# Attention values of two heads in the two column halves of the array, with probabilities moving and y arriving turned

## The reference

```python
# 8 query heads of 64, 2 key/value heads (4 query heads share one), blocks of 128 tokens
# latent tokens see: key blocks t-1, t, t+1 of the latents (|distance| <= 128) + the 256 context keys
# context tokens see: the 256 context keys
s = (q @ k.T) * 64 ** -0.5               # masked
m = max(s, sink); p = exp(s - m)
y = (p @ v) / (sum(p) + exp(sink - m))   # the sink adds to the sum and has no value
...
y_mix = sigmoid(h @ w_gm) * (ym @ w_br_m) + sigmoid(h @ w_ga) * (ya @ w_br_a) + sigmoid(h @ w_gr) * (yr @ w_br_r)
```

## Time and profile before

| | |
|---|---|
| three runs | 2885.79, 2887.33, 2889.2 us |
| median | 2887.33 us |
| span of the profiled execution | 2889.5 us |
| TensorE busy | 2786.0 us (96%) |
| VectorE busy | 1287.6 us (45%) |
| ScalarE busy | 1009.6 us (35%) |
| GpSimd busy | 1113.4 us (39%) |

### The profile page before, as it was taken

The page is one execution under the profiler, slowest core; times in us unless marked ns, Lnnn a source line. Parts: engine busy times, 40 slices in busy tenths (PEclk is TensorE's granted clock), DMA queues, the critical chain, the costliest instruction groups (busy, mean ns, idle before and its releaser), DMA issues. The chain is left out here.

```text
span 2889.5 us, 43951 instructions
## 1 busy us (share of the span) xinstructions
PE 2786.0 (96%) x17300; PEld 2431.1 (84%) x17300; DVE 1287.6 (45%) x2843; ACT 1009.6 (35%) x1864; POOL 1113.4 (39%) x976
## 2 busy tenths in 40 slices
PE   7999899999999998999999999989999999899998
PEld 4888788999998897888888878877988888888887
DVE  4554537524453135333333546645625441344446
ACT  4333236533332224222222343324633332333332
POOL 2333231153333333433433444332153345365555
PEclk9999999999999999999999999999999999999999
DMA  5111210022213143111111331131022222522223
GB/s 236 59 59 62 86 66 23 16 92 88 88 74 117 59 154 124 70 62 59 73 59 59 118 117 59 52 109 67 16 99 97 94 74 85 192 88 102 88 99 112
DMA packets 39370, 249.54 MB, mean 86 GB/s; under 512 B 4480, under 2 KB 4864, under 8 KB 13568
## 3 DMA queue, kind: packets, MB, share of 16 engines
q1 hardware_dynamic: 36288, 236.25, 22.9%
q10 hardware_dynamic: 2880, 10.49, 0.9%
HBM read 236.23 MB, written 10.49 MB: 85 GB/s over the span
## 5 line engine op out<-in xcount | busy, mean ns | idle before, releaser
L2333 POOL TENSOR_TENSOR w_rest<-raw,w_head 128x512 fp32r<-128x512 f32 (+1 forms) x634 | 831.2, 1344 | 930.3 <-ACT w_head L1372 910.7
L941 PE MATMUL psum_products<-h_head,w_head 128*128 128x512 f32 (+2 forms) x2288 | 819.6, 358 | 3.8 <-DVE h_rest L1809 2.2
L941 PE MATMUL psum_products<-h_rest,w_head 128*128 128x512 f32 (+2 forms) x2288 | 803.9, 351 | 0.0
L941 PE MATMUL psum_products<-h_head,w_rest 128*128 128x512 f32 (+2 forms) x2288 | 803.9, 351 | 0.0
L941 PEld LDWEIGHTS psum_products<-h_head,w_head 128*128 128x128 f32 (+1 forms) x2288 | 428.9, 187 | 65.1 <-DVE h_rest L1809 3.4
L941 PEld LDWEIGHTS psum_products<-h_rest,w_head 128*128 128x128 f32 (+1 forms) x2288 | 428.5, 187 | 62.1 <-issue 0.8
L941 PEld LDWEIGHTS psum_products<-h_head,w_rest 128*128 128x128 f32 (+1 forms) x2288 | 429.6, 188 | 57.3 <-issue 1.5
L1372 ACT ACTIVATE w_head<-raw 128x1024 fp32r<-128x1024 f32 (+1 forms) x321 | 320.4, 1044 | 399.6 <-PE psum_products L941 350.7
L941 PE MATMUL psum_products<-w_head,h_head 128*128 128x256 f32 x1408 | 403.5, 287 | 1.6 <-DVE h_rest L1872 1.6
L941 PE MATMUL psum_products<-w_rest,h_head 128*128 128x256 f32 x1408 | 391.7, 278 | 0.0
L941 PE MATMUL psum_products<-w_head,h_rest 128*128 128x256 f32 x1408 | 391.5, 278 | 0.0
(11 more groups left out here) (278 smaller groups left out, 3793.6 us busy)
## 6 DMA issues: line engine op xcount, KB each, us to landing
raw<-in_stream SPq DMA_DIRECT2D x182, 1024.0 KB, 4.8
mods_mid<-in_stream SPq DMA_DIRECT2D x10, 1024.0 KB, 9.6
raw<-in_stream SPq DMA_DIRECT2D x16, 512.0 KB, 3.5
residual<-stage ACTq DMA_DIRECT2D x16, 512.0 KB, 2.6
stage<-residual SPq DMA_DIRECT2D x14, 512.0 KB, 4.7
mods_b<-in_stream SPq DMA_DIRECT2D x5, 1024.0 KB, 24.0
mods_a<-in_stream SPq DMA_DIRECT2D x3, 1024.0 KB, 13.8
x_in<-in_x SPq DMA_DIRECT2D x4, 512.0 KB, 8.7
```

Source lines behind the costliest of these rows:

```text
L941: return nc.tensor.matmul(o, a, b, start=start, stop=stop)
L2333: G.tensor_tensor(wl[:, s["sp"] % 2, a:b], place_of(s)[:, a:b], wh[:, s["sp"] % 2, a:b].bitcast(F32), ALU.subtract).then_inc(*ev.mark("poo ...
```

## The change

The values of two heads are made together. The items are reordered so that head g and head g + 4, which belong to different value heads, follow one another. The value block of 64 columns is now stationary, in the lower half of the array's columns for the first head and in the upper half for the second; the 128 turned probabilities move. The output is y turned: partitions are the 128 columns of y for the two heads, the free dimension is the tokens. So the four transposes of y and their copy go. The reciprocal must now stand along the tokens: VectorE writes it 64 times side by side (128x64 for each head, `a_r_rows`), TensorE turns this 128x128 block once for each pair, ScalarE copies it (`a_r_cols`), and VectorE multiplies the pair's y by it (128x128). `a_pt` gets a third buffer. The rows of `w_br_a` are reordered on the host to match. The loop has n + 3 ticks instead of n + 4.

```diff
-        heads = [(t, hd) for t in tiles for hd in range(AH)]
-        ticks("attend", AH * len(tiles) + 4, fill, 12 * len(pairs(ctx)) - 6, l=l,
-              heads=heads, banks=lambda i: int(tile_ends(heads, i)))
+        heads = [(t, g + 4 * half) for t in tiles for g in range(4) for half in range(2)]
+        ticks("attend", AH * len(tiles) + 3, fill, 12 * len(pairs(ctx)) - 6, l=l, heads=heads)
...
+                        pair = (i_ - 4) // 2 if i_ >= 4 and i_ % 2 == 0 else None
+                        if pair is not None:
+
+                            pe.wait_ge(*ev.at("ard", l, i_ - 3))
+                            pe.wait_ge(*ev.at("apt", l, i_ - 3))
+                            nc.tensor.transpose(psm[:, 3, P:2 * P], arb[:, pair % 2, :], c("ident")).then_inc(
+                                *ev.mark("pe", "arT", l, pair))
...
+                            if i_ >= 5 and i_ % 2:
+                                pe.wait_ge(*ev.at("arc", l, (i_ - 5) // 2))
...
-                        if 3 <= i_ <= n + 2:
...
-                            for m, kt_ in enumerate(keys):
-                                last = mm(psm[:, 4, 0:AD], apt[:, j % 2, m * P:(m + 1) * P],
-                                          av[:, kt_, lo:lo + AD], m == 0, m == len(keys) - 1)
-                            last.then_inc(*ev.mark("pe", "apv", l, j))
...
+                        if pair is not None:
+                            t, _ = st["heads"][2 * pair]
+                            pe.wait_ge(*ev.at("apt", l, 2 * pair + 1))
+                            if pair >= 1:
+                                pe.wait_ge(*ev.at("ay", l, pair - 1))
+                            keys = akeys(t)
                             for m, kt_ in enumerate(keys):
+                                for half in range(2):
+                                    lo = half * AD
+                                    last = mm(psm[lo:lo + AD, 4, 0:P], av[:, kt_, lo:lo + AD],
+                                              apt[:, (2 * pair + half) % 3, m * P:(m + 1) * P],
+                                              m == 0, m == len(keys) - 1)
+                            last.then_inc(*ev.mark("pe", "apv", l, pair))
...
+                        if i_ >= 4 and i_ % 2 == 0:
+
+                            pair = (i_ - 4) // 2
+                            act.wait_ge(*ev.at("arT", l, pair))
+                            if pair >= 1:
+                                act.wait_ge(*ev.at("ay", l, pair - 1))
+                            nc.scalar.activation(arc[:], psm[:, 3, P:2 * P], ACT.Copy).then_inc(
+                                *ev.mark("act", "arc", l, pair))
...
-                            V.reciprocal(small[:, s2 + 5:s2 + 6], small[:, s2 + 4:s2 + 5]).then_inc(
+                            pair, half = divmod(i_ - 2, 2)
+                            if pair >= 2:
+                                dve.wait_ge(*ev.at("arT", l, pair - 2))
+                            V.reciprocal(arb[:, pair % 2, half * AD:half * AD + AD],
+                                         small[:, s2 + 4:s2 + 5].broadcast_to((P, AD))).then_inc(
                                 *ev.mark("dve", "ard", l, i_ - 2))
...
-                            V.tensor_scalar(ay[:, t % 2, hd * AD:(hd + 1) * AD], psm[:, 4, 0:AD],
-                                            small[:, s0 + 5:s0 + 6], None, ALU.mult).then_inc(
-                                *ev.mark("dve", "ay", l, j))
+                        if i_ >= 4 and i_ % 2 == 0:
+                            pair = (i_ - 4) // 2
+                            t, hd = st["heads"][2 * pair]
+                            dve.wait_ge(*ev.at("apv", l, pair))
+                            dve.wait_ge(*ev.at("arc", l, pair))
+
+                            V.tensor_tensor(ya[:, t, hd, :], psm[:, 4, 0:P], arc[:], ALU.mult).then_inc(
+                                *ev.mark("dve", "ay", l, pair))
```

More of the change, by code:

```diff
@@ L110, in param_places @@
     return place, n
-def tile_ends(heads, i):
-    return i >= 4 and heads[i - 4][1] == AH - 1
 def make_plan():
@@ L685, in backbone @@
         kh, kr = [Region(6 * 1024 * i)(n, [P, 2, TOK], F32R) for i, n in enumerate(("a_k_head", "a_k_rest"))]
-        R = Region(12 * 1024 + 64)
-        ya = Region(R.off)("a_y_turned", [P, TILES - 1, 4, P])
+        R = Region(12 * 1024)
+        ya = Region(R.off)("a_y_turned", [P, TILES, 4, P])
         qs = R("a_q_split", [P, TILES, AH, P], F32R)
@@ L691, in backbone @@
         asb = R("a_s", [P, 3, 640])
-        apt = R("a_pt", [P, 2, 640])
-        ay = R("a_y", [P, 2, 512])
+        apt = R("a_pt", [P, 3, 640])
+        arb = R("a_r_rows", [P, 2, P])
+        arc = R("a_r_cols", [P, P])
         tga = R("a_tg", [P, 3, 2, TOK])
@@ L903, in yT_of @@
         def yT_of(br, kt, t):
-            if br != "a" or t == TILES - 1:
+            if br != "a":
                 return yT[:, 0:kt, t * P:(t + 1) * P]
@@ L1586, in _ @@
                             act.wait_ge(*ev.at("apT", l, j))
-                            if j >= 2:
-                                act.wait_ge(*ev.at("apv", l, j - 2))
-                            nc.scalar.activation(apt[:, j % 2, 0:n1], psm[:, 2, 0:n1], ACT.Copy).then_inc(
+                            if j >= 3:
+                                act.wait_ge(*ev.at("apv", l, (j - 3) // 2))
+                            nc.scalar.activation(apt[:, j % 3, 0:n1], psm[:, 2, 0:n1], ACT.Copy).then_inc(
                                 *ev.mark("act", "apt", l, j))
                             if nk > 512:
-                                nc.scalar.activation(apt[:, j % 2, 512:640], psm[:, 3, 0:P], ACT.Copy).then_inc(
+                                nc.scalar.activation(apt[:, j % 3, 512:640], psm[:, 3, 0:P], ACT.Copy).then_inc(
                                     *ev.mark("act", "apt", l, j))
+                        if i_ >= 4 and i_ % 2 == 0:
[5 more added lines that the diff above has]
+                                *ev.mark("act", "arc", l, pair))
                         if i_ < n:
@@ L1605, in _ @@
                                                      *ev.mark("act", "ap", l, i_))
[L1606 to L1612, removed]
                 elif kind == "rqk_sb":
@@ L2442, in layout @@
         w = g[name][s["l"], row:row + s["kt"] * P]
+        if name == "w_br_a":
+            w = w.reshape(2, 4, AD, -1).transpose(1, 0, 2, 3).reshape(4 * P, -1)
         w = np.concatenate([w[:, a:a + n] for a, n in cols], 1)
```

7 lines of the change are left out of this document (removed).

## The result

The changed kernel takes 2896.14 us (median of 10 runs, 2893.86 to 2900.85) against 2887.75 us for the one before (10 runs, 2885.79 to 2892.13). The ratio is 1.0027, with a 95% interval of 1.0019 to 1.0034: it is slower by 8.4 us.

A forecast was written before the change was run, and what follows sets the result against it. TensorE was taken to set the pace: work of -20.1 us and waits of +30.8 us sum to +10.7 us, which on the earlier kernel's median of 2887.3 gives 2898 us; range 2880 to 2912.

The forecast's parts named there:

- A value record at 0.055: TensorE's value products: each of 640 new records takes 0.055 us with two halves at once, 35.2 us in all.
- The switch at 0.33: TensorE entering and leaving the split array: 0.33 us for each of 40 pairs, less 0.08 already paid, 10.0 us.
- nearly free: Rival at the value groups: 0.046 us a record and no switch cost, sum -8.3 us, 2879 us; chance 0.17.
- dear: Rival at the value groups: loads bound them, 0.08 us a record, switch dearer, 16 us more, 2914 us; chance 0.08.
- no overlap: Rival at the value products: halves don't run together, 0.11 us a record, 35 us more, 2933 us; chance 0.08.
- The work at -20.1: TensorE's work: 65.3 us of value records removed, 35.2 added, 10.0 for switches, together -20.1 us.
- The reciprocal: VectorE's reciprocal, 64 elements instead of one: 7 ns for each further element, 0.48 us more, about 0.63 in all.
- rival of a cheap reciprocal: Rival at VectorE's wide reciprocal: 7 ns is scatter, 24 waits are 0.48 us shorter, no change, 2887 us; chance 0.15.
- The wait: Odd ticks without weight piece: the reciprocals' transpose starts 2.62 us after scores end (T), TensorE ready at 1.20, waiting 1.42.
- Where: Second attention stretch some 11 us longer, with 14 of the 22 waits; the first about as long as before.
- Weight loads: TensorE's full-row loads of 64 columns: under the skill's rule they don't overlap products, another 41 us, 2939 us.
- Under cover: ScalarE's added block copies, ahead of an exponential needed two ticks later, are hidden by TensorE's 93.9 of 97 us against 63.7.

The follow-up runs named there:

- e4_turn: Changed kernel with all value products of the lower half made first, then the upper half's, instead of alternating: 2913.94 us, ratio 1.0082 to the kernel before.
- e7_before_odd: Kernel before the change, with its weight pieces placed behind odd ticks first: 2892.42 us, ratio 1.0012 to the kernel before.
- e5_behind_odd: Changed kernel with weight pieces behind odd ticks first and the transpose of the reciprocals moved behind the values: 2870.23 us, ratio 0.9936 to the kernel before.
- e1_narrow: Changed kernel with the reciprocal writing one of its 64 columns, the others constant (y not the reference's): 2885.27 us, ratio 0.999 to the kernel before.
- e2_odd: Changed kernel with a weight piece behind every odd tick and the remainder behind even ones: 2872.77 us, ratio 0.9942 to the kernel before.

## Why the prediction was right

2898.0 was forecast and 2896.14 came, by the mechanism forecast. The number alone would not show it, since the range of 2880 to 2912 also held no change at all (2887); the waits, their place and the experiments do. Step by step:

- **A value record at 0.055.** The group of 20 lasts from 2053.74 to 2054.99, 1.25 us; 20 x 0.055 and the lag of 0.13 behind it are 1.23. Groups of 8, 16 and 20 (0.59, 1.02, 1.25) separate the two: 0.055 a record, and a lag of 0.15. e4_turn shows that groups of 16 and 20 need the halves to alternate for this.
- **The switch at 0.33.** Ahead of the group the five transposes take 0.64 (2053.10 to 2053.74) instead of 0.55, so 0.09. With 0.15 behind it, and 0.34 from the first weight product to the second where the next takes 0.23, so 0.11, the three lags read from quarters of the array return with halves, 0.35 together. The rivals that priced the halves otherwise (nearly free, dear, no overlap) fall with these two.
- **The work at -20.1.** TensorE's busy time fell by 12.0 in records whose ends are modelled, and some of it passed at the lower clock, which settles little. e7_before_odd against e5_behind_odd gives 22.2, with the waits left and the slow clock about even.
- **The reciprocal.** The tile's row in the changed kernel (shortest/median/longest ns):

```profile
L2215 DVE RECIPROCAL a_r_rows<-small x80: 535/543/553, 438.0 to 2099.5; 128x64 f32<-128x64 f32 x80
```

  543 - 153 = 390 ns for 63 elements are 6.2 ns each; 7 had been read. The added time is 0.39 us where I had 0.48. The Trainium skill (VectorE: DVE Perf Modes, "First, the fixed hardware budget"), read as eight cycles an element, gave an estimate of 0.53 for the added time; the trace is below that. The rival of a cheap reciprocal was wrong in its premise, and e1_narrow shows what it would have given: 2885 us, where it said 2887.
- **The wait.** The transpose of the reciprocals starts at T + 2.46 where T + 2.62 was forecast: 0.09 of the difference is the reciprocal, 0.09 the way from VectorE to TensorE (0.06, not 0.15). VectorE's start (T + 0.20) and its 1.66 us up to the reciprocal were as read. The wait is then 1.26, not 1.42. It divides into 0.70 ahead of the scores (shown as 0.53) and 0.56 ahead of the transpose (shown as 0.40). Twenty-two waits shorter by 0.16 are 3.5 us, which would make the forecast +7.2; +8.4 was measured.
- **Where.** +11 was forecast for the second layer and nothing for the first; +9.5 and, with the clock up, -1.7 came. The sizes differ by about what the wait was over-read: 14 x 0.16 = 2.2 and 8 x 0.16 = 1.3. VectorE was forecast busy for some 80 us in the second stretch; it is 72.6.
- **Weight loads.** In the second window loads are busy for 66.17 us and products for 81.33, in 97: together half as much again as the window. Full-row loads do overlap products here. The Trainium skill (TensorE: Matmul & The Clock Gate, Part 3: Packing small matmuls) lets a load overlap only when its row group differs; this trace doesn't bear that out, and the 41 us that this rule would add did not appear.

What the prediction did not see is how far ScalarE's weight conversions reach, and that the clock can fall behind the waits at a loop's end (1.5 us in the profiled execution). "Under cover" holds for the changed kernel, but once pieces stand in odd ticks, ScalarE's copies are late (6.2 us of waits in e2_odd, 8.7 in e5_behind_odd). Ten of these twelve waits stand behind two weight conversions; placing them elsewhere wasn't tried, so what that would give is open.

## What to carry to other kernels

Work of two items merged into one tick leaves the other tick empty: ask what engine was running under the work that left, and put filler there (here moving weight pieces turned +8 us into -15, with not one instruction less). A cost on a second engine is worth what its cover leaves open: 0.39 us of reciprocal was worth 11 us over 80 heads where only some ticks were covered, and nothing measurable where all odd ticks were. When a change and a placement interact, measure all four combinations, since the placement alone made the old kernel about 4 us slower. When two loops are compared, check that both ends stand behind the same work and at the same clock: here this moved 8.0 to 9.5.

## What the hardware showed

- Two products in the two column halves overlap all along when they alternate (0.055 us a record of 64 stationary and 128 moving float32 columns; 8, 16 and 20 records take 0.59, 1.02 and 1.25). One half after the other overlaps only for about 0.4 us of a group, and each further record costs 0.11 (0.60, 1.51 and 1.95).
- A reciprocal costs 6.2 ns for each further element of a partition (128x1: 153 ns, 128x64: 543 ns).
- Entering and leaving the split array costs about 0.35 us, spread over three places: 0.09 ahead, 0.15 behind, 0.11 in the first product behind.
- At the lower clock level a weight product of 512 moving columns took 0.43 us from start to start instead of 0.23 (559.11 to 559.54 in the changed kernel). The clock fell behind a wait of 2.6 us in one execution and stayed up behind 2.7 in another of the same kernel.
